# Two transformer blocks on one core: other byte offsets in SBUF for the split weights and the 256-column activations

## The chip, the cores and the metric

The kernel runs on one core of one Trainium2 chip. The metric is the time of one execution on the device in microseconds (us); where several runs are given, their median. An offset below is a byte address within a partition of SBUF, taken modulo 256 bytes, unless it is said otherwise: "at 64" means 64, 320, 576 and so on.

## The reference, cut to what matters

A sequence of 256 positions (272 with 16 meta tokens in front) of width 2048 goes through two blocks. The first has neighbourhood attention and latent attention side by side and a gated MLP with a short convolution (5632 wide); the second has a convolution branch and a gated linear recurrence, both gated into a merge, and a gated MLP (5632 wide), with shifts and gains that come from a conditioning vector (`w_ada_2`). Nearly all the arithmetic is products with large weight matrices in float32:

```python
proj = rmsnorm(h, mix_norm_g[l]) @ w_in[l]              # 2048 x 3904
h = h + mix @ w_out[l]                                  # 2048 x 2048
return (jax.nn.silu(gc) * u) @ w_down                   # g, u = x @ w_gate, x @ w_up; 2048 x 5632, 5632 x 2048
proj = h @ w_in[l]                                      # second block, 2048 x 11264
y_a = (a_b * conv(a_c * a_x)) @ w_conv_out[l]           # 1024 x 2048
y_b = o @ w_hgrn_out[l]                                 # 1024 x 2048
x = x + gt_m * (merged @ w_o[l])                        # 2048 x 2048
ff = (jax.nn.silu(h2 @ w_ffn_gate[l]) * (h2 @ w_ffn_up[l])) @ w_ffn_down[l]
```

## The kernel before

Activations are kept transposed: features on the 128 partitions, positions along the columns. Every weight matrix is cut into slabs of 2048 float32 columns per partition (1 MB): for a group of 256 output features, 8 blocks of 128 input features. `make_plan` (line 115) writes the list of all slabs and products; all engines walk it in the same order.

**A slab's way.** The SP queue loads it into `raw` (three buffers, line 626). ScalarE rounds it, half a slab at a time, to the high part `wh` (line 1301); VectorE subtracts to get the low part `wl` (line 1811). Both have three buffers. Activations are split alike: each operand tile has two halves, `[:, 0]` the high and `[:, 1]` the low part.

**A product.** `gemm` (line 681) goes over the 128-row blocks k of the slab and over two output tiles j of 128 features each. For each k and j it issues three matmuls that add up into one PSUM bank:

```python
pe.matmul(dst, h[:, c, o:o + w], x[:, 0, k, g.t0:g.t1], start=(k == 0), stop=False)    # line 704
pe.matmul(dst, h[:, c, o:o + w], x[:, 1, k, g.t0:g.t1], start=False, stop=False)       # line 705
m = pe.matmul(dst, l[:, c, o:o + w], x[:, 0, k, g.t0:g.t1], start=False, stop=end)     # line 706
```

The second argument is the stationary operand (128 weight columns of `wh` or `wl`, loaded by an own instruction, PEld in the profile), the third the moving one (256, 258 or 272 columns of activations). `gemm_raw` (line 643) does the same with unscaled activations (lines 671 to 673), `gemm_by_head` (line 712) for two small products (lines 732 to 734). Between slabs' quarters, `lanes.pump` lets generators issue the small matmuls and transposes of attention, of the recurrence (`hgrn`, lines 984 to 1022) and of the conditioning vector (`ada`, line 806); they wait in the same queue of TensorE.

**Places.** `sb` gives tiles one place behind the other, and the first, `raw0`, begins at byte 16512, at 128 of 256. `raw` and `wh` take whole multiples of 256, so every `wh` buffer starts at 128. Behind `wh` stand three rows of 272 floats (`rstd`, `ssq_h`, `ssq_a`: 3264 bytes, 192 over a multiple of 256), so every `wl` buffer starts at 64. A weight tile k, j lies 1024 k + 512 j bytes into its buffer and so at its buffer's offset. `row_home` (line 323) moves a tile to a wanted offset: the 256-column operands (`xs` of the second block's projections, gate and up products and `w_o`; `hid` of both down products; `conv` and `oo`) start at `wh_off + 64`, which is 192; their rows are 1024 bytes long, so every row k of both halves starts at 192. The operands of the first block (`xx`, and `xb`, `cqx`, `ckvx`, `raw_in`, `raw_ffn`) have rows of 272 floats, 1088 bytes, so that from one k to the next the offset moves on by 64 and comes round every four. `xx` starts at 64; its matmuls take columns from 14 on (258 columns), from 16 on (256 columns, start offsets 128, 192, 0, 64 for k = 0, 1, 2, 3, then again) or from 0 (272).

Of the kernel before, what the change touches and what calls it, by code (L numbers as in the profile page):

```python
# [8 lines left out]
F32R = mybir.dt.float32r  # L9
# [4 lines left out]
P = 128  # L14
D = 2048
KD = D // P
META = 16
SEQ = 256
T = META + SEQ
# [9 lines left out]
ROW_BYTES = 256  # L29
# [276 lines left out]
def build(nc, A, out):  # L306
    ctx = ExitStack()
    with ctx:
        base = (nc.sbuf_base + 31) // 32 * 32
        limit = nc.sbuf_usable_end  # L310
        cursor = [base]

        def at(name, shape, dt, offset):
            size = 4 * int(np.prod(shape[1:]))
            assert offset + size <= limit, (name, offset, size, limit)
            return nc.alloc_sbuf_tensor_at(name, shape, dt, offset=offset), offset + size

        def sb(name, shape, dt=F32):
            t, cursor[0] = at(name, shape, dt, cursor[0])
            cursor[0] = (cursor[0] + 31) // 32 * 32  # L320
            return t

        def row_home(offset, place):
            return offset + (place - offset) % ROW_BYTES
# [4 lines left out]
        raw = [sb(f"raw{i}", [P, SLAB]) for i in range(NR)]  # L329
        wh_off = cursor[0]  # L330
        wh = [sb(f"wh{i}", [P, SLAB], F32R) for i in range(NS)]
        rstd = sb("rstd", [P, T])
        ssq = {n: sb(f"ssq_{n}", [P, T]) for n in "ha"}
        assert (cursor[0] - wh_off) % ROW_BYTES == 192
        wl = [sb(f"wl{i}", [P, SLAB], F32R) for i in range(NS)]
        xoff = cursor[0]
        xx = sb("xx", [P, 2, KD, T], F32R)
        xs, _ = at("xs", [P, 2, KD + 1, SEQ], F32R, row_home(xoff, wh_off + 64))
        hoff = cursor[0]
        H = sb("H", [P, KD, T])  # L340
        cst = sb("cst", [P, NCONST])
# [5 lines left out]
        nx_off = cursor[0]  # L347
        nx = [sb(f"nx{i}", [P, T]) for i in range(NXB)]
        sqt = [sb(f"sqt{i}", [P, T]) for i in range(2)]
        ssq["b"] = sb("ssq_b", [P, T])  # L350
        ada_off = cursor[0]
        ada_raw = [sb(f"ada_raw{i}", [P, 512]) for i in range(NADA)]
        ada_acc = sb("ada_acc", [P, 512])
# [1 line left out]
        arena = cursor[0]  # L355
# [30 lines left out]
        out_a, _ = at("out_a", [P, 8, T], F32, hoff)  # L386
        out_b, _ = at("out_b", [P, 8, T], F32, hoff + 8 * T * 4)
# [2 lines left out]
        assert off <= mla_end  # L390

        raw_in, _ = at("raw_in", [P, 2, KD, T], F32R, limit // 32 * 32 - 8 * KD * T)
        ffn_home = row_home(arena, wh_off + 64)
        raw_ffn = [at(f"raw_ffn{i}", [P, 2, 8, T], F32R, ffn_home + (2 + 22 * i) * SEQ * 4)[0] for i in range(2)]
        raw_mix, _ = at("raw_mix", [P, 2, 6, T - Q0], F32R, ffn_home + 2 * HALF * SEQ * 4)
        cursor[0] = ffn_home
        hid = sb("hid", [P, 2, HALF, SEQ], F32R)
        gct = [sb(f"gc{i}", [P, SEQ]) for i in range(NGC)]

        cursor[0] = mix_home = row_home(arena, wh_off + 64)  # L400
        conv = sb("conv", [P, 2, 8, SEQ], F32R)
        cursor[0] = oo_home = row_home(cursor[0], wh_off + 64)
        oo = sb("oo", [P, 2, 8, SEQ], F32R)
        cu = sb("cu", [P, 2, SEQ])
        cy = sb("cy", [P, 2, SEQ])
# [6 lines left out]
        masks32, _ = at("masks32", [P, nmask], F32, oo_home)  # L412
# [2108 lines left out]
def program(nc, arrays):  # L2521
    aps = {n: nc.dram_tensor(f"in_{n}", list(a.shape), mybir.dt.from_np(a.dtype), kind="ExternalInput").ap()
           for n, a in arrays.items()}
    out = nc.dram_tensor("out_0", [D, SEQ], F32, kind="ExternalOutput").ap()
    build(nc, aps, out)
# [13 lines left out]
```

## Time and profile before

| | |
|---|---|
| Runs | 2701.0, 2701.86, 2703.86 us; median 2701.86 |
| Profiled execution | 2700.86 us, span of its instructions 2699.5 us |
| TensorE matmul (PE), weight load (PEld) | busy 98% and 97% of the span, 22052 instructions each |
| VectorE (DVE), ScalarE (ACT), GpSimd (POOL) | busy 68%, 46%, 12% |
| Granted TensorE clock, mean | 0.995 of full speed (2.4 GHz) |
| DMA | 571.22 MB, mean 212 GB/s |

Matmuls are pipelined: one is shown some 280 ns long, but the next starts some 116 ns after it. So the distance from one start to the next tells the rate, not the length of one. Views used below: the page, groups of instructions by line and shape, stretches of the span with counts, waits, the chain of work that ended last, and the timeline.

### The profile page before, as it was taken

The page shows a single profiled execution, that of the slowest core. Times are in us where ns is not written, and L with a number is a line of the kernel's source. Part 1 is how long each engine was busy: PE and PEld are TensorE (multiplying, and loading weights), DVE is VectorE, ACT ScalarE, POOL GpSimd, SP SyncE. Part 2 cuts the span into 40 slices and gives each one's busy share as a digit, 9 for nine tenths or more (in the row PEclk, how much of TensorE's full clock was granted, in tenths as well). Part 3 has the DMA queues.
Part 4 walks back from the last instruction along what each step waited for, and adds up shares of the span by engine and source line. Part 5 has one row for each costly group of instructions (what it writes and reads, how often), then busy time and mean ns, then how long its engine had stood idle before and what let it go on. Part 6 is the DMA issues. An engine that isn't in the chain of part 4 may idle for free.

```text
span 2699.5 us, 51384 instructions
## 1 busy us (share of the span) xinstructions
PE 2645.3 (98%) x22052; PEld 2606.7 (97%) x22052; DVE 1844.0 (68%) x2592; ACT 1248.4 (46%) x1943; POOL 331.5 (12%) x526
## 2 busy tenths in 40 slices
PE   7999999999999999999999999999999999999998
PEld 7888889999999999999999999999999999999998
DVE  6666568877777777787888667776877644444444
ACT  5556655544433444445444443334554443444443
POOL 2110101111121111231000001110211000000001
PEclk9999999999999999999999999999999999999999
DMA  6433345678788887886444568886768656555553
GB/s 204 137 106 103 118 148 173 205 267 269 263 293 278 277 270 262 272 285 207 152 147 155 188 225 279 273 279 217 256 208 273 219 192 191 195 188 190 187 186 126
DMA packets 500084, 571.22 MB, mean 212 GB/s; under 512 B 26704, under 2 KB 473424, under 8 KB 499856
## 3 DMA queue, kind: packets, MB, share of 16 engines
q1 hardware_dynamic: 467968, 463.76, 52.6%
q0 software_dynamic: 31600, 103.80, 11.9%
q8 instruction: 174, 2.85, 0.4%
q10 hardware_dynamic: 288, 0.36, 0.1%
q14 instruction: 54, 0.44, 0.0%
HBM read 565.77 MB, written 2.54 MB: 211 GB/s over the span
## 4 chain that ended last, share of the span: by engine, by line
PE 86%; DVE 7%; ACT 4%; issue 1%; DMA 1%; POOL 0%; SPq 0%; DVEq 0%; ACTq 0%
PE ps L704 27%; PE ps L705 27%; PE ps L706 26%; DVE wl L1811 3%; ACT wh L1301 2%; PE ps L1002 1%; PE ps L833 1%; DMA raw<-in_w_in 1%; DVE nx L1915 1%; DVE lr L2007 1%; ACT lp L1476 0%; PE ps L806 0%; PE ps L858 0%; PE ps L859 0%; PE ps L671 0%
## 5 line engine op out<-in xcount | busy, mean ns | idle before, releaser
L1811 DVE TENSOR_TENSOR wl<-raw,wh 128x1024 fp32r<-128x1024 f32 (+1 forms) x894 | 1058.9, 1200 | 577.0 <-ACT wh L1301 572.7
L1301 ACT ACTIVATE wh<-raw 128x1024 fp32r<-128x1024 f32 (+1 forms) x894 | 883.2, 1030 | 606.1 <-PE ps L706 587.8
L704 PE MATMUL ps<-xs,wh 128*128 128x256 f32 x2880 | 811.3, 282 | 5.8 <-DVE xs L1892 5.8
L705 PE MATMUL ps<-xs,wh 128*128 128x256 f32 x2880 | 799.4, 278 | 0.0
L706 PE MATMUL ps<-xs,wl 128*128 128x256 f32 x2880 | 796.7, 277 | 0.0
L704 PEld LDWEIGHTS ps<-xs,wh 128*128 128x128 f32 x2880 | 539.9, 187 | 7.6 <-DVE wl L1811 5.8
L705 PEld LDWEIGHTS ps<-xs,wh 128*128 128x128 f32 x2880 | 545.0, 189 | 1.0 <-issue 1.0
L706 PEld LDWEIGHTS ps<-xs,wl 128*128 128x128 f32 x2880 | 539.5, 187 | 0.0
L704 PE MATMUL ps<-xx,wh 128*128 128x258 f32 (+3 forms) x1840 | 530.2, 288 | 3.7 <-DVE xx L1894 3.7
L705 PE MATMUL ps<-xx,wh 128*128 128x258 f32 (+3 forms) x1840 | 522.3, 284 | 0.0
L706 PE MATMUL ps<-xx,wl 128*128 128x258 f32 (+3 forms) x1840 | 522.3, 284 | 0.0
L704 PE MATMUL ps<-hid,wh 128*128 128x256 f32 x1408 | 393.4, 279 | 0.0
L705 PE MATMUL ps<-hid,wh 128*128 128x256 f32 x1408 | 390.1, 277 | 0.0
L706 PE MATMUL ps<-hid,wl 128*128 128x256 f32 x1408 | 388.8, 276 | 0.0
L704 PEld LDWEIGHTS ps<-xx,wh 128*128 128x128 f32 (+1 forms) x1840 | 347.9, 189 | 8.8 <-DVE wl L1811 3.7
L1162 POOL DMA_DIRECT2D ada_raw<-in_w_ada x384 | 206.7, 538 | 1193.4 <-DVE ada_acc L2060 1055.7
L705 PEld LDWEIGHTS ps<-xx,wh 128*128 128x128 f32 (+1 forms) x1840 | 348.3, 189 | 0.7
L706 PEld LDWEIGHTS ps<-xx,wl 128*128 128x128 f32 (+1 forms) x1840 | 347.5, 189 | 0.0
L2060 DVE SCALAR_TENSOR_TENSOR ada_acc<-ada_raw,small,ada_acc 128x512 f32<-128x512 f32 x360 | 268.4, 746 | 0.0
L705 PEld LDWEIGHTS ps<-hid,wh 128*128 128x128 f32 x1408 | 266.2, 189 | 0.0
L704 PEld LDWEIGHTS ps<-hid,wh 128*128 128x128 f32 x1408 | 263.4, 187 | 0.0
L706 PEld LDWEIGHTS ps<-hid,wl 128*128 128x128 f32 x1408 | 263.3, 187 | 0.0
(378 smaller groups left out, 2753.2 us busy)
## 6 DMA issues: line engine op xcount, KB each, us to landing
raw<-in_w_in SPq DMA_DIRECT2D x118, 1024.0 KB, 5.3
ada_raw<-in_w_ada POOLq DMA_DIRECT2D x384, 256.0 KB, 4.8
raw<-in_w_gate SPq DMA_DIRECT2D x44, 1024.0 KB, 6.5
raw<-in_w_up SPq DMA_DIRECT2D x44, 1024.0 KB, 7.1
raw<-in_w_ffn_gate SPq DMA_DIRECT2D x44, 1024.0 KB, 5.2
raw<-in_w_ffn_up SPq DMA_DIRECT2D x44, 1024.0 KB, 5.3
raw<-in_w_down SPq DMA_DIRECT2D x32, 1024.0 KB, 6.0
raw<-in_w_ffn_down SPq DMA_DIRECT2D x32, 1024.0 KB, 5.4
```

What stands on the lines that cost most here:

```text
L704: pe.matmul(dst, h[:, c, o:o + w], x[:, 0, k, g.t0:g.t1], start=(k == 0), stop=False)
L705: pe.matmul(dst, h[:, c, o:o + w], x[:, 1, k, g.t0:g.t1], start=False, stop=False)
L706: m = pe.matmul(dst, l[:, c, o:o + w], x[:, 0, k, g.t0:g.t1], start=False, stop=end)
L833: m = pe.matmul(bank[0:w, 0:keys_of(j)], l[:, o:o + w], r[:, 0:keys_of(j)], start=(i == 0), stop=(i == len(qk) - 1))
L1002: m = pe.matmul(bank[:, 128 * j:128 * j + 128], k[:, n, 128 * b:128 * b + 128], q[:, n, 128 * b:128 * b + 128], start=True, stop=True)
L1162: pool.dma_start(ada_raw[i % NADA][:, :], w[:, k, 512 * g:512 * g + 512]).then_inc(s_ada[i % NADA], 16)
L1301: act.activation(wh[i % NS][:, part], raw[i % NR][:, part], ACT.Copy).then_inc(s_hi, 1)
L1811: dve.tensor_tensor(wl[i % NS][:, part], raw[i % NR][:, part], wh[i % NS][:, part].bitcast(F32), ALU.subtract).then_inc(s_lo, 1)
L1915: dve.scalar_tensor_tensor(out=x, in0=norm_src(n, i), scalar=norm_gain(n, i), in1=rstd[:, 0:m], op0=ALU.mult, op1=ALU.mult).then_inc(s_nx, 1)
L2007: dve.reciprocal(r[:, :], r[:, :]).then_inc(s_ldve[lane], 1)
L2060: dve.scalar_tensor_tensor(out=ada_acc[:, :], in0=r, scalar=s, in1=ada_acc[:, :], op0=ALU.mult, op1=ALU.add).then_inc(s_acc, 1)
```

## The change

Five edits of places. The three rows between `wh` and `wl` move behind `sqt`; so `wl` follows `wh` at once and starts at 128 as `wh` does. The 256-column operands go from `wh_off + 64` to `wh_off - 64`, from 192 to 64. By the same edits, `xx` and `H` start at 128 in place of 64 (3264 bytes further down), `raw_ffn` and `raw_mix`, which are placed from `ffn_home`, move by 128 bytes (from 192 to 64), and what stands between `xx` and `sqt` (`H`, constants, vectors, masks, `small`, `nx`) moves down by 3264 bytes. `raw`, `wh`, `xb`, `cqx`, `ckvx`, `raw_in`, the `ada` tiles and the start of the arena stay. No instruction, wait or order changes.

```diff
         wh = [sb(f"wh{i}", [P, SLAB], F32R) for i in range(NS)]
-        rstd = sb("rstd", [P, T])
-        ssq = {n: sb(f"ssq_{n}", [P, T]) for n in "ha"}
-        assert (cursor[0] - wh_off) % ROW_BYTES == 192
+        assert (cursor[0] - wh_off) % ROW_BYTES == 0
         wl = [sb(f"wl{i}", [P, SLAB], F32R) for i in range(NS)]
         xoff = cursor[0]
         xx = sb("xx", [P, 2, KD, T], F32R)
-        xs, _ = at("xs", [P, 2, KD + 1, SEQ], F32R, row_home(xoff, wh_off + 64))
+        xs, _ = at("xs", [P, 2, KD + 1, SEQ], F32R, row_home(xoff, wh_off - 64))
...
         sqt = [sb(f"sqt{i}", [P, T]) for i in range(2)]
-        ssq["b"] = sb("ssq_b", [P, T])
+        rstd = sb("rstd", [P, T])
+        ssq = {n: sb(f"ssq_{n}", [P, T]) for n in "hab"}
...
-        ffn_home = row_home(arena, wh_off + 64)
+        ffn_home = row_home(arena, wh_off - 64)
...
-        cursor[0] = mix_home = row_home(arena, wh_off + 64)
+        cursor[0] = mix_home = row_home(arena, wh_off - 64)
         conv = sb("conv", [P, 2, 8, SEQ], F32R)
-        cursor[0] = oo_home = row_home(cursor[0], wh_off + 64)
+        cursor[0] = oo_home = row_home(cursor[0], wh_off - 64)
         oo = sb("oo", [P, 2, 8, SEQ], F32R)
```

## Rows read from the trace of the kernel before

**Rows 1.** The page: span, and busy time of each engine.

```profile
span 2699.5 us, 51384 instructions
PE 2645.3 (98%) x22052; PEld 2606.7 (97%) x22052; DVE 1844.0 (68%) x2592; ACT 1248.4 (46%) x1943; POOL 331.5 (12%) x526
```

**Rows 2.** The page: the chain that ended last, by engine.

```profile
PE 86%; DVE 7%; ACT 4%; issue 1%; DMA 1%; POOL 0%; SPq 0%; DVEq 0%; ACTq 0%
```

**Rows 3.** Groups by line and shape, TensorE: busy us, mean ns, idle before.

```profile
L704 PE MATMUL ps<-xs,wh 128*128 128x256 f32 x2880 | 811.3, 282 | 5.8 <-DVE xs L1892 5.8
...
L704 PE MATMUL ps<-hid,wh 128*128 128x256 f32 x1408 | 393.4, 279 | 0.0
...
L706 PE MATMUL ps<-xx,wl 128*128 128x258 f32 x896 | 253.9, 283 | 0.0
...
L706 PE MATMUL ps<-xx,wl 128*128 128x256 f32 x672 | 188.5, 281 | 0.0
...
L704 PE MATMUL ps<-conv,wh 128*128 128x256 f32 x128 | 35.8, 280 | 0.0
L704 PE MATMUL ps<-oo,wh 128*128 128x256 f32 x128 | 35.7, 279 | 0.0
```

**Rows 4.** Timeline of TensorE, second down product: 100 rounds of three.

```profile
2220.10 0.28 PE L704 MATMUL ps<-hid,wh 128*128 128x256 f32 x1
2220.22 0.28 PE L705 MATMUL ps<-hid,wh 128*128 128x256 f32 x1
2220.33 0.28 PE L706 MATMUL ps<-hid,wl 128*128 128x256 f32 x1
2220.44 0.28 PE L704 MATMUL ps<-hid,wh 128*128 128x256 f32 x1
...
2254.76 0.28 PE L704 MATMUL ps<-hid,wh 128*128 128x256 f32 x1
```

**Rows 5.** Timeline of TensorE, an up product of the first block: 96 matmuls.

```profile
644.68 0.28 PE L704 MATMUL ps<-xx,wh 128*128 128x256 f32 x1
...
647.13 0.28 PE L704 MATMUL ps<-xx,wh 128*128 128x256 f32 x1
...
647.49 0.28 PE L704 MATMUL ps<-xx,wh 128*128 128x256 f32 x1
...
656.00 0.28 PE L704 MATMUL ps<-xx,wh 128*128 128x258 f32 x1
```

**Rows 6.** Timeline of TensorE, a gate and up product of the second block.

```profile
2002.99 0.28 PE L704 MATMUL ps<-xs,wh 128*128 128x256 f32 x1
...
2026.67 0.28 PE L704 MATMUL ps<-xs,wh 128*128 128x256 f32 x1
```

**Rows 7.** Timeline of TensorE, just behind eight matmuls of the recurrence.

```profile
1303.29 0.28 PE L704 MATMUL ps<-xs,wh 128*128 128x256 f32 x1
...
1303.65 0.28 PE L704 MATMUL ps<-xs,wh 128*128 128x256 f32 x1
1303.77 0.28 PE L705 MATMUL ps<-xs,wh 128*128 128x256 f32 x1
1303.88 0.28 PE L706 MATMUL ps<-xs,wl 128*128 128x256 f32 x1
1304.00 0.28 PE L704 MATMUL ps<-xs,wh 128*128 128x256 f32 x1
```

**Rows 8.** Stretches: engines' busy us (count), granted clock, DMA share, GB/s.

```profile
600.00:800.00 200.00, 200.00 (x1704) 200.00 (x1703) 152.11 (x204) 84.22 (x108) 36.55 (x68) 1.00 0.82 273
2220.00:2320.00 100.00, 100.00 (x868) 100.00 (x867) 49.21 (x53) 36.29 (x39) 0.00 (x0) 1.00 0.59 187
```

**Rows 9.** Waits of TensorE and of the weight split, by total.

```profile
PE ps L671 <- DVE wl L1811: 15.0, 2, 14.1
...
ACT wh L1301 <- PE ps L706: 587.8, 219, 4.9
DVE wl L1811 <- ACT wh L1301: 572.7, 337, 6.8
```

## The prediction

> **What bounds the kernel now.** I read the page first: TensorE is busy for 98% of a span of 2699.5 us, with 22,052 matmuls and as many weight loads [rows 1], and it holds 86% of the chain that ended last [rows 2]. The waits come next: the longest of TensorE is 15.0 us at the start, on the first `wl`, while the split of the weights itself waits for TensorE (587.8 us at line 1301) and its second half for its first (572.7 us) [rows 9]. Everything else is ahead of TensorE; what changes the time is the distance from one matmul's start to the next one's. The change touches just that or nothing, for it alters no instruction.
>
> The stretches give that distance at full clock: 868 matmuls in 100 us of the second down product, 1704 in 200 us of the first block's gate and up products [rows 8], 115 and 117 ns each. The reader is to see that the two differ although the engine was at its full clock in both. The timeline says why not shape alone. In the second down product 300 matmuls of 256 columns take 2254.76 − 2220.10 = 34.66 us, 115.5 ns each, and their rounds of three (lines 704, 705, 706) last 346.6 ns, in steps of about 118, 116 and 113 ns [rows 4]. An up product of the first block has the same 256 columns and the same weight tiles in the same buffers, and its 96 matmuls take 656.00 − 644.68 = 11.32 us, 117.9 ns each [rows 5]. What differs is the activation's offset: always 192 in the first case, going round 128, 192, 0, 64 in the second. While a matmul streams, the next one's weights are loaded, and where the two streams start against each other shows in the rate. **An offset is worth up to 2.4 ns a matmul here**, 2%.
>
> Against that stands a rule of the Trainium skill, SBUF — State Buffer, section "Who interferes with whom": TensorE has one read port for the moving operand and an independent one for weights, and "PE and ACT never wait on anyone". By that rule this change is worth 0 us, and both stretches would run alike. The trace does not agree: 115.5 against 117.9 ns.
>
> **The change part by part.** Call an operand's offset less the offset of the weights loaded beside it the lead.
>
> 1. *256-column operands.* Before, the lead is 192 − 128 = 64 in two of the three steps (weights from `wh`) and 192 − 64 = 128 in the third (from `wl`). After, it is 64 − 128 = −64, that is 192, in all three. How many matmuls: 2880 + 1408 + 128 + 128 = 4544 rounds [rows 3], 13,632 matmuls. All lie on the path, with nothing beside them that could hide a longer or shorter step. So each ns per round is 4.5 us.
>
> What does a round cost at lead 192? The nearest rows are in the up product at k = 3, where the activation is at 64: its second tile's round, in which two of three weight loads have lead 192 and the third lead 0, goes from 647.13 to 647.49, 0.36 us by the rounded times [rows 5]. A second reading is better resolved. With the old offsets too the engine has a second rhythm into which it falls by chance of entry: from 2002.99 to 2026.67 it runs 67 rounds in 23.68 us, 353.4 ns each, 117.8 ns a matmul [rows 6]. That is 6.8 ns over the usual round, and it fits the 0.36 us of k = 3 and the up product's mean of 117.9 (353.8 ns a round). The shape of these rows is that rounds settle at a few lengths, 346.6 and 353.4 ns, and stay there. I take 353.4 ns for the new layout, because the only rows with this operand at 64 show it and because the old round is the shortest in the trace, so that most other placements must be longer. The old kernel already runs the 67 rounds of that row in the longer rhythm, so 4544 − 67 = 4477 rounds pay 353.4 − 346.6 = 6.8 ns: **+30 us**.
>
> Bounds. Lower: the three steps become one kind; if it were the shortest of the old three, 113 ns (2220.33 to 2220.44), a round is 339 ns, −7.6 ns × 4477 = −34 us. Upper: behind an interruption a round from 1303.29 to 1303.65 takes 360 ns before the rhythm is back (the next takes 350) [rows 7]; if the new layout stayed there, (360 − 346.6) × 4544 = +61 us.
>
> 2. *First block's products.* Rows there go round all four offsets against `wh` before and after, whatever the start of `xx`, so their two `wh` loads of three see the same four leads. The `wl` loads see the same four leads too, in another order. Line 706 has 896 and 672 of them [rows 3], with some 700 more of other shapes, 2,300 in all; its mean lengths, 283 and 281 ns, are within 3 ns of its neighbours' at every shape. I take 0; with ±1 ns for a changed order, ±2 us.
>
> 3. *Splitting.* ScalarE and VectorE write `wh` and `wl` for 894 half slabs each. `wl` is written at another offset. Any change of their length lies under TensorE: they wait for it in total 587.8 us and for each other 572.7 us [rows 9]. 0 us. Without that cover, 1% of the 1058.9 us of line 1811 would be 11 us.
>
> 4. *DMA.* The destination `raw` does not move. 0 us. If TensorE gets faster, a slab is wanted sooner: 48 matmuls at 113 ns are 5.4 us in place of 5.5 for 1 MB. At 273 GB/s and a share of 0.82 in the densest stretch [rows 8] there is room for 2% more; late next would be the slab behind the `ada` loads.
>
> 5. *Small tiles* (`rstd`, `ssq`, `nx`, constants) move; they feed VectorE, ScalarE and some hundred small matmuls. In the recurrence both operands move together, so its lead stays 0. 0 us, ±1.
>
> The sum against the profiled execution: 2700.9 + 30 = 2731 us; its time is 1 us under the median of the runs, so the number for a median is 2732, and as the entry into a rhythm is partly chance I put 2731.
>
> [...]
>
> **The rivals.**
>
> *A, faster.* With one lead in all three steps the uneven rhythm has no cause any more, and the even one that takes its place could be a shorter one: each step 113 ns, as the shortest now. Lengths seem to settle at distinct values 6.8 ns a round apart (346.6, 353.4, 360); the next below is 339.8, −6.8 × 4477 = −30 us: 2671 us. For it: at lead 64 the trace shows both the 118 and the 113 ns step, so the lead alone does not set a step, and the order of leads does. Against it: no round of 339.8 stands anywhere in the trace, not even in the first block, whose operands pass through every lead. It decides for "faster" as soon as a round is under 345.4 ns (5.4 us over 4544 rounds).
>
> *B, much slower.* The even rhythm is 120 ns, the 360 ns round of the interruptions: +61 us, 2762 us. For it: the rows show that this round occurs with aligned operands [rows 7]. Against: the first block's mean over all leads is 117.9.
>
> *C, no change.* Either the offset counts only by whether it is the same in every row (1024-byte rows stay as they are, 1088-byte rows as they were), or the old 346.6 ns round comes back at the new lead: 2701 us. For it: what sets the two rates apart in the trace is equally well "same offset each k" against "another each k", which the change leaves alone. Against: the second rhythm with the same offsets shows that sameness alone does not give 346.6.
>
> **How the numbers follow.** Forecast (353 ns a round or close by): 0.39, 2731 us. A: 0.31. B: 0.13. C: 0.17. A measurement of this kernel tells about 0.2% (5.4 us) from no change. Faster 0.31, same 0.17, slower 0.52. Cases of both signs hold most of the chance. The forecast's own range is 2720 to 2742; the one for 8 in 10 must take in A with its bound of −34 us (2668) and B with +61 (2763).
>
> **What would show it.** Right: in the second down product the timeline shows rounds of 353 ns and 849 matmuls in 100 us in place of 868; the up product stays at 117.9; waits stay as they are. The even rhythm would show as three equal steps in place of 118, 116, 113. Wrong: rounds at 340 (A), 347 (C) or 360 (B). Wrong in another way: the first block's pace changes by over 1 ns, which would mean that the order of the leads counts there, or a wait of TensorE on line 1811 grows beyond 15 us, which would mean that splitting got slower and has lost its cover.

## The result, and the profile after

Six runs of the changed kernel lie between 2707.76 and 2713.90 us, median **2711.11 us**; six of the kernel before, on the same chip, have a median of 2702.37. The ratio is 1.0028, 95% interval 1.0015 to 1.0041: slower by 0.28%, 8.7 us. The forecast was +30 us. Below, every ratio is against the kernel before, run beside the kernel in question, with its 95% interval. The profiled execution took 2707.76 us, at a mean granted clock of 0.995, as before.

The changed kernel's file is one line shorter above the products, so its line 703 is line 704 of the kernel before, and so on. Its page: span, busy time of each engine, and the chain that ended last.

```profile
span 2706.4 us, 51384 instructions
PE 2652.8 (98%) x22052; PEld 2614.3 (97%) x22052; DVE 1843.8 (68%) x2592; ACT 1248.9 (46%) x1943; POOL 331.1 (12%) x526
...
PE 87%; DVE 7%; ACT 4%; issue 1%; DMA 1%; POOL 0%; SPq 0%; DVEq 0%; ACTq 0%
```

Waits of the changed kernel that answer to [rows 9]: releaser, total us, count, longest. They differ by about 1%, and no more: the split of the weights is as well covered as it was.

```profile
ACT wh L1300 <- PE ps L705: 595.0, 220, 4.9
DVE wl L1810 <- ACT wh L1300: 579.0, 338, 6.8
...
PE ps L670 <- DVE wl L1810: 14.9, 2, 14.4
```

So the span's 6.9 us lie on TensorE, whose busy time grew by 7.5 us (2645.3 to 2652.8). Its groups by line show next to nothing of them, because the length of one matmul is not the distance to the next: 811.4 us after, 811.3 before, and 394.8 against 393.4 [rows 3].

```profile
L703 PE MATMUL ps<-xs,wh 128*128 128x256 f32 x2880 | 811.4, 282 | 5.9 <-DVE xs L1891 5.9
...
L703 PE MATMUL ps<-hid,wh 128*128 128x256 f32 x1408 | 394.8, 280 | 0.0
```

The stretches show them. Those of the changed kernel, in order: first block's gate and up products with the start of the first down product (from 723.5 us on), a part of the first down product, the second down product, and a part of it that every experiment below has in common. Columns as in [rows 8]; a count takes in the two matmuls already running at a stretch's start.

```profile
600.00:800.00 200.00, 200.00 (x1712) 200.00 (x1711) 153.11 (x204) 83.67 (x107) 36.60 (x69) 1.00 0.83 275
732.00:762.00 30.00, 30.00 (x267) 30.00 (x266) 22.28 (x29) 11.21 (x12) 6.45 (x12) 1.00 0.90 297
2220.00:2320.00 100.00, 100.00 (x851) 100.00 (x851) 47.27 (x51) 35.62 (x39) 0.00 (x0) 1.00 0.60 187
2240.00:2310.00 70.00, 70.00 (x596) 70.00 (x596) 33.61 (x38) 24.16 (x27) 0.00 (x0) 1.00 0.61 190
```

And those of the kernel before that were not shown yet:

```profile
732.00:762.00 30.00, 30.00 (x262) 30.00 (x261) 22.20 (x28) 10.70 (x13) 6.45 (x12) 1.00 0.88 293
2240.00:2310.00 70.00, 70.00 (x608) 70.00 (x607) 34.77 (x38) 25.45 (x28) 0.00 (x0) 1.00 0.62 198
```

In one and the same kind of product, with the clock at full speed in both, the changed kernel is faster in one stretch (267 against 262) and slower in another (596 against 608). The timeline of TensorE in the changed kernel shows the two rates, in the first down product. Twice four small transposes (line 805, those of `ada`) break in. From the first break to the second, rounds of three last 0.34 us; behind the second they last 0.36 us.

```profile
726.21 0.60 PE L805 MATMUL ps<-cst,ada_acc 128*128 128x128 f32 x4
...
727.01 0.28 PE L703 MATMUL ps<-hid,wh 128*128 128x256 f32 x1
...
727.35 0.28 PE L703 MATMUL ps<-hid,wh 128*128 128x256 f32 x1
...
768.15 0.28 PE L703 MATMUL ps<-hid,wh 128*128 128x256 f32 x1
...
768.49 0.28 PE L703 MATMUL ps<-hid,wh 128*128 128x256 f32 x1
...
768.83 0.60 PE L805 MATMUL ps<-cst,ada_acc 128*128 128x128 f32 x4
...
769.62 0.28 PE L703 MATMUL ps<-hid,wh 128*128 128x256 f32 x1
769.74 0.28 PE L704 MATMUL ps<-hid,wh 128*128 128x256 f32 x1
769.86 0.28 PE L705 MATMUL ps<-hid,wl 128*128 128x256 f32 x1
769.98 0.28 PE L703 MATMUL ps<-hid,wh 128*128 128x256 f32 x1
```

All 4544 rounds of the 256-column operands are in the trace. Of them 4477 are followed at once by another round (that this is also the prediction's 4544 − 67 is chance); those I measured, from the start of the first matmul of a round to that of the next round. This tally is from the trace's start times, in ns; a round counts for the length from which it is at most some 2.5 ns away:

| kernel | 340.0 | 346.7 | 353.3 |
|---|---|---|---|
| before | 0 | 4224 | 122 |
| after | 1351 | 2 | 3039 |

The rest are mostly the first rounds behind an interruption, and rounds with a wait in them. The old leads have two lengths as well, 346.7 and 353.3, but no 340. A 340 round has three even steps (113, 113, 114 ns), a 353 round too (118, 118, 117). In the kernel after, from 2070.6 us to the end of the last product, all 1756 measured rounds are at 353.3, but for the first one or two behind the one break in it. Priced against 346.7: (3039 − 122) × 6.6 = +19.3 us and 1351 × 6.7 = −9.1 us, together +10.2; the sum over all rounds gives +9.5. The first block gives back 3.4 us, and all small matmuls together take 0.5 us more (the transposes of `ada`, 96 of them, 8.6 us in both kernels). These make 6.6 of the span's 6.9 us.

What the first block gives back shows in the up product of [rows 5]: its 96 matmuls took 11.33 us before and take 11.23 now, 118.0 and 117.0 ns each.

```profile
643.66 0.28 PE L703 MATMUL ps<-xx,wh 128*128 128x256 f32 x1
...
654.89 0.28 PE L703 MATMUL ps<-xx,wh 128*128 128x258 f32 x1
```

Over the whole block, the mean step between two matmuls of one shape that follow each other directly goes from 118.0 to 116.8 ns at 256 columns, from 119.9 to 119.6 at 258 and from 125.2 to 125.0 at 272. That prices its 7344 matmuls at −3.9 us.

### The profile page after: what moved, and what is told of

It is laid out like the page before. It is cut to its first block, busy times and chain, and to the rows that moved or that the text cites. A ratio compares the mean times of both kernels' runs of the same rounds, so it can differ in the third digit from the quotient of the medians.

```text
span 2706.4 us, 51384 instructions
## 1 busy us (share of the span) xinstructions
PE 2652.8 (98%) x22052; PEld 2614.3 (97%) x22052; DVE 1843.8 (68%) x2592; ACT 1248.9 (46%) x1943; POOL 331.1 (12%) x526
## 4 chain that ended last, share of the span: by engine, by line
PE 87%; DVE 7%; ACT 4%; issue 1%; DMA 1%; POOL 0%; SPq 0%; DVEq 0%; ACTq 0%
PE ps L703 27%; PE ps L704 27%; PE ps L705 27%; DVE wl L1810 3%; ACT wh L1300 1%; PE ps L1001 1%; PE ps L832 1%; DMA raw<-in_w_in 1%; DVE nx L1914 1%; DVE lr L2006 1%; PE ps L848 0%; PE ps L805 0%; PE ps L857 0%; PE ps L858 0%; PE ps L670 0%
## 5 line engine op out<-in xcount | busy, mean ns | idle before, releaser
L703 PE MATMUL ps<-xs,wh 128*128 128x256 f32 x2880 | 811.4, 282 | 5.9 <-DVE xs L1891 5.9
L705 PE MATMUL ps<-xs,wl 128*128 128x256 f32 x2880 | 804.8, 279 | 0.0
L703 PE MATMUL ps<-hid,wh 128*128 128x256 f32 x1408 | 394.8, 280 | 0.0
L705 PE MATMUL ps<-hid,wl 128*128 128x256 f32 x1408 | 394.4, 280 | 0.0
```

## The experiments

**Which part of the change costs.** The changed kernel has two edits, the place of `wl` and the place of the 256-column operands. Each was made alone.

`e1_wl_only`: only `wl` moves, and with it `xx` and the small tiles, as in the change (leads 64, 64, 64).

```diff
# the changed kernel, at its four places
-row_home(xoff, wh_off - 64)
+row_home(xoff, wh_off + 64)
```

> Low weights at 128 (as in the changed kernel), 256-column activations left at 192: the lead is 64 in all three steps. Theory (the offsets fix which round lengths exist, the entry picks among them): with one lead for all steps the three steps become equal or the rounds split into two lengths as in the changed kernel; the 346.6 ns round with steps of 118, 116, 113 is gone, and the total is somewhere between 2671 (all 340) and 2731 us (all 353). Rival (only the activations' move to 64 matters): rounds of 346.6 ns as before, 2702 us within 5 us.

Measured: 2729.69 us, ratio 1.0100 (1.0084 to 1.0115). 4357 rounds at 353.3, 42 at 340. The up product of [rows 5] takes 117.0 ns a matmul, as in the changed kernel.

`e2_x_only`: only the operands move (leads 192, 192, 0).

```diff
# the kernel before, at its four places
-row_home(xoff, wh_off + 64)
+row_home(xoff, wh_off - 64)
```

> 256-column activations at 64, low weights left at 64: leads 192, 192, 0. Theory (lengths belong to the set of leads, not to the place of the activations alone): other round lengths than in the changed kernel, no three equal steps of 113 ns. Rival (the activations' place alone sets the lengths): the same two lengths of 340 and 353 ns as in the changed kernel, about 2711 us. If only the new low-weight place counted, rounds would be 346.6 and the time 2702.

Measured: 2730.35 us, ratio 1.0104 (1.0089 to 1.0119). 4368 rounds at 353.3, none at 340; 25 lie between 346 and 349. The theory had expected other lengths than those of the changed kernel; what came is one of its two. The up product of [rows 5] takes 118.0 ns a matmul, as before the change: its gain comes with the new places of `wl` and `xx`.

The stretch 2240 to 2310 of `e1_wl_only`, then of `e2_x_only`:

```profile
2240.00:2310.00 70.00, 70.00 (x597) 70.00 (x596) 33.55 (x36) 24.47 (x27) 0.00 (x0) 1.00 0.58 181
```

```profile
2240.00:2310.00 70.00, 70.00 (x597) 70.00 (x596) 33.04 (x35) 26.42 (x28) 0.00 (x0) 1.00 0.59 185
```

Each half alone costs 27 or 28 us, about what I had forecast for the whole; both together cost 9. The halves do not add up: what counts is the set of leads that comes out. An even lead (`e1_wl_only`) does not keep the 340 round, though it has it in 42 rounds.

**Other leads.** In the changed kernel the four places get another offset each; all three leads are equal.

```diff
-row_home(xoff, wh_off - 64)     # lead 192, the changed kernel
+row_home(xoff, wh_off)          # e3_lead0
+row_home(xoff, wh_off + 128)    # e4_lead128
+row_home(xoff, wh_off - 32)     # e10_lead_224
+row_home(xoff, wh_off - 96)     # e11_lead_160
```

> Both weights and the activations at 128: lead 0 in all three steps. Theory (a uniform lead allows even steps, multiples of a 6.67 ns beat per round): again equal steps and lengths out of 340.0, 346.7, 353.3, 360.0 ns, the mix set by entry; 2671 to 2762 us. Rival (banks collide outright at lead 0): every round at 360 ns or more, 2760 us or above. Rival (the lead does not matter, only the same place each row): 2702 to 2711 us.

Measured: 2757.91 us, ratio 1.0204 (1.0187 to 1.0221); 4342 rounds at 360, in three steps of 120. The rival that expected every round at 360 ns or more came out, its 2760 us missed by 2. The round that stood in the old trace only behind interruptions [rows 7] is here the rule:

```profile
2240.00:2310.00 70.00, 70.00 (x586) 70.00 (x585) 33.36 (x38) 26.30 (x29) 0.00 (x0) 1.00 0.58 184
```

> Both weights at 128, activations at 0: lead 128 in all three steps. Theory: even steps or two lengths, multiples of 6.67 ns, another share of each than in the changed kernel; 2671 to 2762 us. Rival (only sameness counts): 2702 to 2711 us.

Measured: 2741.55 us, ratio 1.0142 (1.0127 to 1.0157); rounds of 351 to 355 (some 2500) and of 359 to 361 ns (some 1900), mixed.

> The changed kernel with the 256-column activations at 96 in place of 64: lead 224 in all steps, the first run off the 64-byte grid. Theory in its strict form (lengths are multiples of 6.67 ns at any lead): rounds of 340.0 to 360.0 ns on that grid. Rival (streams that start off a 64-byte line touch one line more): all rounds at 360 ns or more, 2760 us or above, as the 258-column operands of the first block are at 359 to 361 ns a round.

Measured: 2735.53 us, ratio 1.0120 (1.0106 to 1.0134).

> The changed kernel with the 256-column activations at 32: lead 160 in all steps. The same two expectations as at lead 224; if the lead counted smoothly, between the 2711 us of lead 192 and the 2742 us of lead 128.

Measured: 2731.86 us, ratio 1.0109 (1.0095 to 1.0123). In these two the rounds spread from 350 to 361 ns and keep to no single length, so the strict form of the theory (multiples of 6.67 ns at any lead) is refuted, and so is the rival of 360 ns or more. Both times lie between those of the neighbouring leads (0 and 192, 128 and 192), as they would if the lead counted smoothly. None of the four leads beats 192, and only at 192 do long stretches of 340 appear.

**Is it the lead or the place?** `e5_all_up_64` moves every tile of the changed kernel up by 64 bytes, but for `raw_in` of the first block, which is placed from the end of SBUF.

```diff
-base = (nc.sbuf_base + 31) // 32 * 32
+base = (nc.sbuf_base + 31) // 32 * 32 + 64
```

> The changed kernel with every tile 64 bytes higher (the first begins at 64 more): weights at 192, 256-column activations at 128; all leads as in the changed kernel. Theory (only the difference of the offsets counts): rounds of 340.0 and 353.3 ns and nothing else, 2711 us within 6 us (the shares may differ by entry). Rival (the absolute offset counts, each stream has good and bad places of its own): other lengths, and a time as far away as the other layouts', 2730 us or above.

Measured: 2709.44 us over 12 runs, ratio 1.0008 (0.9989 to 1.0027); in the profiled one 1390 rounds at 340 and 3006 at 353.3, the mixture of the changed kernel almost to the round. So at this shift, the only one tried, the leads decide and the places do not. But three of the twelve runs took 2688.9, 2691.6 and 2692.3 us: the same program can come out some 18 us faster. Those runs have no trace.

**What picks 340 or 353?** In the trace of the kernel after, the length changes only where something breaks in (other matmuls, the start of such operands, a wait) and in the one or two rounds behind that. `e6_probe_entries` puts one of eight kinds of extra work, into an unused bank of PSUM, ahead of each slab of the second MLP's later half and of both down products.

```diff
# the changed kernel, in gemm
+if key[0] == 2 and (key[1] == "down" or key[2] == 1):
+    kick(kicks[0] * 5 % 8)
+    kicks[0] += 1
```

> The changed kernel with an additional small piece of TensorE work, of eight kinds in turn, ahead of every slab of the second MLP's second half and of its down products (92 places); their results go to an unused PSUM bank, so only the entry into the following rounds changes. Theory (the entry picks the rhythm, which then stays): both lengths follow, the next 6 or more rounds keep one length, and some kinds lead to 340 more often than others; the 512-column float32 matmul, which in the trace of the changed kernel was followed by 340 in 4 of 4 cases, leads to 340 again. Rival (the rhythm is set by what VectorE, ScalarE and the DMA queues do at that time, not by the entry): the length changes with no relation to the kind, and within runs of rounds.

Measured, one run: 2732.86 us. Rounds behind each piece, from the trace:

| extra work | from 340 | from 353 |
|---|---|---|
| float32, 512 columns | 353: 6 | 353: 6 |
| two transposes | 353: 11 | |
| one transpose | 340: 6, 353: 5 | |
| three transposes | | 340: 12 |
| float32, 256 columns | | 340: 6, 353: 5 |
| float32, 128 columns | 340: 12 | |
| float32r, 384 columns | 340: 12 | |
| float32r, 512 columns | 340: 6 | 340: 5 |

The float32 matmul of 512 columns, expected to lead to 340, led to 353 in all 12 cases. Two kinds led from one length to either. The kinds follow each other in a fixed order, so most met one length only. Here the last kind breaks in (line 693) on rounds of 0.36 us and leaves rounds of 0.34:

```profile
2276.97 0.28 PE L725 MATMUL ps<-hid,wh 128*128 128x256 f32 x1
...
2277.32 0.28 PE L725 MATMUL ps<-hid,wh 128*128 128x256 f32 x1
...
2277.68 0.40 PE L693 MATMUL ps<-xs 128*128 128x512 f32 x1
...
2278.27 0.28 PE L725 MATMUL ps<-hid,wh 128*128 128x256 f32 x1
...
2278.61 0.28 PE L725 MATMUL ps<-hid,wh 128*128 128x256 f32 x1
```

Both lengths are therefore states of the same instructions at the same offsets. Behind a piece that breaks in one or the other sets in, and it holds until the next. The kind of the piece alone does not fix which.

`e7_steer_3` puts a float32 matmul of 512 columns at three places where the changed kernel was at 353.

```diff
+if key in [(2, "down", 0, 0), (2, "gate", 1, 0), (2, "down", 1, 0)]:
+    kick()
```

> The changed kernel with one 512-column float32 matmul into an unused PSUM bank ahead of three places of the second MLP (first down product, second half's first gate product, second down product). Each costs about 0.86 us (428 + 27 + 518 ns in place of 118, by the recurrence's matmul of that shape). Theory: some 1400 of the rounds behind the first go from 353.3 to 340.0 ns, -13.3 ns each, -18.6 us, less 2.6 us: about 2695 us, faster than both kernels. If a second such matmul throws a stretch back into 353, about 2705. Rival (the entry doesn't set the rhythm): 2711 + 3 = 2714 us.

Measured: 2708.72 us, ratio 1.0023 (1.0014 to 1.0032). A miss: two of the three led to 353, one to 340 (for 349 rounds). All three met 353, so what a piece does depends on more than its kind and the length that it meets.

`e8_reentry` takes the one kind that had led to 340 from either length (now on `wh` in place of `xs`), and puts it, 24 times, at the first 256-column round behind the transposes of `ada`, behind those of the recurrence, and where such operands begin.

```diff
# the changed kernel, in gemm; retime is set behind ada's and the recurrence's transposes
+if retime[0] and even[0]:
+    retime[0] = False
+    pe.matmul(PX[0][:, 0:512], wh[i % NS][:, 0:128], wh[i % NS][:, 0:512], start=True, stop=True)
```

> The changed kernel, which at the first round with a 256-column operand behind each group of transposes of the conditioning vector, behind the recurrence's transposes and where such operands begin, issues one 512-column float32r matmul on the slab at hand into an unused PSUM bank (some 35 of them). In the run with eight kinds of entry, this piece was followed by the 340 ns round in 11 of 11 cases, from either length. Theory (the entry picks the length and the length stays): at least 85% of the rounds at 340.0 ns; 3039 rounds were at 353.3, so up to -40 us, plus 35 x 0.25 = 9 us: about 2680 us, 0.8% faster than the kernel before. Rival (these lengths come and go by what the other engines do): shares as in the changed kernel, 2720 us.

Measured: **2677.89 us**, ratio 0.9914 (0.9902 to 0.9927), with 24 more matmuls than the changed kernel. 4060 rounds at 340 (91%), 343 at 353.3. Behind 19 of its 24 pieces the rounds are at 340, behind five at 353.3, one of these five from 340. From 2067.9 us to the end every round is at 340, but for the first behind a break. Its page, the two stretches, and one piece (line 709) in the timeline:

```profile
span 2680.9 us, 51432 instructions
PE 2626.1 (98%) x22076; PEld 2585.4 (96%) x22076; DVE 1843.8 (69%) x2592; ACT 1249.1 (47%) x1943; POOL 330.6 (12%) x526
```

```profile
2220.00:2320.00 100.00, 100.00 (x884) 100.00 (x884) 48.66 (x52) 37.07 (x42) 0.00 (x0) 1.00 0.63 202
2240.00:2310.00 70.00, 70.00 (x620) 70.00 (x619) 35.67 (x39) 26.80 (x29) 0.00 (x0) 1.00 0.60 190
```

```profile
1591.98 0.60 PE L815 MATMUL ps<-cst,ada_acc 128*128 128x128 f32 x4
1592.34 0.48 PE L709 MATMUL ps<-wh 128*128 128x512 f32 x1
...
1593.01 0.28 PE L713 MATMUL ps<-xs,wh 128*128 128x256 f32 x1
...
1593.35 0.28 PE L713 MATMUL ps<-xs,wh 128*128 128x256 f32 x1
```

The changed kernel has (3039 − 343) more rounds at 353.3; times 13.3 ns that is 36 us, less some 24 × 0.3 us for the pieces: 29. Measured between the medians, on two chips: 33; by the two ratios: 31; between the two profiled executions: 25.5, with 4.5 us lost in the first 728 us, whose instructions and places are the same in both kernels.

`e9_reentry_before` is the control: the same 24 matmuls in the kernel before.

> The kernel before with the same added matmuls at the same places. Theory: at its leads (64, 64, 128) the trace shows 346.7 ns nearly throughout and no 340, so an entry has nothing to pick; the added work costs 9 us: 2711 us. Rival (the added matmul itself speeds what follows, whatever the offsets): under 2700 us.

Measured: 2708.16 us, ratio 1.0021 (1.0012 to 1.0031). 4336 rounds at 346.7, 31 at 353.3, none at 340:

```profile
2240.00:2310.00 70.00, 70.00 (x608) 70.00 (x608) 34.44 (x36) 25.84 (x28) 0.00 (x0) 1.00 0.58 184
```

So the pieces gain nothing by themselves, they cost their own 6 us. They only change which of the lengths sets in that the leads make possible; with the old leads no 340 was seen. The pieces were not tried with the leads of `e1_wl_only`, which had 340 in 42 rounds.

`e12_other_reentry` has at the same 24 places another piece, one that had led to 353 every time in `e6_probe_entries`.

```diff
-pe.matmul(PX[0][:, 0:512], wh[i % NS][:, 0:128], wh[i % NS][:, 0:512], start=True, stop=True)
+for q in range(2):
+    pe.transpose(PX[0][:, 128 * q:128 * q + 128], wh[i % NS][:, 128 * q:128 * q + 128].bitcast(F32), ident)
```

> The same places as the re-entry kernel (24 of them), but two 128-column float32 transposes in place of the one 512-column float32r matmul; in the run with eight kinds of entry two transposes were followed by the 353 ns round in 11 of 11 cases (all from 340). Theory (the entry alone picks the length): hardly any round at 340, nearly all at 353.3: against the changed kernel 1351 rounds x 13.3 ns = +18 us and 24 x 0.2 = 5 us: about 2733 us, although the added work is shorter than that of the re-entry kernel with 2678 us. Rival (any added piece of work there helps): 2680 to 2700 us. If two transposes lead to either length when they come on top of a 353 stretch, in between, some 2720 us.

Measured: 2677.94 us, median of five, as fast as `e8_reentry` where I had expected it as slow as the 353 rounds make it. Its profiled execution took 2718.97 us; the other four took 2675.5 to 2683.3, and their ratio is 0.9917 (0.9901 to 0.9934). In that one 3290 rounds are at 353.3 and 1098 at 340; had all of the 3290 been at 340, it would have been 3290 × 13.3 ns = 44 us shorter, 2675, which is where the others lie. Their rounds were not recorded, so that they ran at 340 is inferred from their time. In the recorded one two transposes were followed by 340 in 12 cases and by 353 in 12, where they had led to 353 in 11 of 11 in `e6_probe_entries`. So the kind of the piece is not what fixes the result, and the same program can differ by over 40 us from one execution to the next.

## Why the prediction was half right

**What bounds the kernel: right.** Only distances between starts changed. Waits, the split, the chain and the clock are as they were.

**Step 1, 256-column operands: right in kind, wrong in size.** The failed step is "I take 353.4 ns for the new layout", for all 4477 rounds. The price of such a round was right: 3039 rounds do run at 353.3, and each is 6.6 ns longer than the old one, where 6.8 was forecast. But 1351 rounds, 30%, run at 340.0, rival A's length, which has no row in the trace before. The term of +30 us measured +9.5. That the kernel came out slower, as forecast, is in part luck: with the share of 340 that `e8_reentry` has, the same leads give a faster one. I had read [rows 6] rightly as a second length "by chance of entry" and then gave the new layout only one. A row that shows one operand layout at two lengths says that another layout may have two as well; the sum should have been a share of each.

The argument for 353.4 was weak too. The round it was read off has leads 192, 192 and 0 [rows 5], and a layout that keeps these leads does run at 353.3 (`e2_x_only`). The new layout has 192 in the third step as well, which no row showed, and there 340 occurs. And "the old round is the shortest in the trace, so that most other placements must be longer" held for the six other sets of leads tried (nearly all rounds between 350 and 361 ns), and not for the one in question.

**Step 2, first block's products: wrong, and small.** The step was "I take 0", with ±2 us for the changed order of the leads. The order counts: 117.0 ns a matmul in the up product in place of 118.0, −3.9 us for the block by its mean steps. Before, the leads of a round were L, L and L + 64; now they are L, L and L. This is the prediction's own sign of being wrong "in another way", a first block that changes its pace by over 1 ns: 118.0 to 116.8 at 256 columns. Its stretch of 200 us with 1704 matmuls [rows 8] was also read wrongly as gate and up products alone; its last 75 us are the first down product; from 600 to 723.5 us there are 1042, one in 118.7 ns.

**Steps 3 and 4, splitting and DMA: right**, 0 us. The 15.0 us that the prediction calls the longest wait is the total of two, the longest of them 14.1 [rows 9]; now they are 14.9 and 14.4. **Step 5, small tiles: right**, 0 ± 1 expected, +0.5 measured.

**The rivals.** A's mechanism, "each step 113 ns", exists, with its three even steps, and had it held everywhere, 2671 us would have been near: `e8_reentry` reaches 2677.9 with 24 added matmuls. B's round of 360 belongs to lead 0 (`e3_lead0`, 2757.9 us against B's 2762). C's first form, that an offset counts only by being the same in every row, falls with the spread from 2711 to 2758 us over layouts that are all the same in every row; its second, that 346.6 comes back, with 2 such rounds.

**The rule of the Trainium skill** in SBUF — State Buffer, "Who interferes with whom", by which the change is worth 0 us, does not agree with these runs: with nothing but offsets changed, the time goes from 2711 to 2758 us.

**Open.** Why 340 or 353 sets in behind a break was not settled: two predictions of it (`e7_steer_3`, `e12_other_reentry`) missed. Nor is it shown whether the two streams, weights and activations, contend for anything, or why equal leads that go round gain in the first block while equal leads of 64 that stay lose in the second.

## What to carry to other kernels

Where matmuls run back to back, measure the distance from one start to the next stretch by stretch before and after a change of places; the busy share (98% in both kernels) and the length of one matmul hide it, and a mean over the kernel can be two rhythms mixed. A layout that looks slightly worse may hold the fastest rhythm for part of the time: look for stretches that became faster, and try what else picks the rhythm before the layout is dropped (here 2711 became 2678 us with 24 extra matmuls, 0.9% under the kernel before). Since one program can come out at either, take several runs, and a profile beside each time if you can.

## What the runs showed of the hardware that I had not expected

- The offset of the moving operand against that of the stationary one decides which steps of a 256-column float32r matmul occur, from 113.3 ns (lead 192, `e8_reentry`) to 120 ns (lead 0, `e3_lead0`), at a granted clock of 1.00 in both. Moving both by 64 bytes changed neither the lengths nor the median (`e5_all_up_64`).
- In the first block, whose offsets go round from row to row, it was enough to bring `wl` to the same offset as `wh`: 118.0 to 117.0 ns a matmul (the kernel before and `e2_x_only` against the changed kernel and `e1_wl_only`).
- With offsets in steps of 64 bytes, nearly all round lengths are 340.0, 346.7, 353.3 and 360.0 ns, that is 51, 52, 53 and 54 times 6.67 ns (lead 128 has many 1 or 2 ns off these). At offsets 32 bytes off that grid (`e10_lead_224`, `e11_lead_160`) the lengths leave it. What beats at 6.67 ns no run shows.
- One instruction sequence has two stable rhythms, and keeps the one into which it fell: over 1600 rounds in a row without a break, 0.55 to 0.57 ms, at 353.3 in the changed kernel and at 340 in `e8_reentry`.
- Extra work can make a kernel faster: 24 matmuls cost 6 us in one layout and gained 33 in the other.
- One program's time can differ by 1.6% from one execution to the next (`e12_other_reentry`, 2675.5 and 2719.0 us) at the same granted clock, 0.994 and 0.995.
